# Attention scores on reversed query rows: the relative bias moves from TensorE to VectorE, two kinds of transfer move to GpSimd's queue, and every weight split is done in halves

## What is computed

```python
xn = _rmsnorm(h, norm_mix_g)
p_rw, q, c_kv, iq, ik, iw, gates = _split(xn @ w_in, IN_SPLITS)
# RWKV branch: each token's projection is mixed with that of the token before it
prev = jnp.pad(p, ((0, 0), (1, 0), (0, 0)))[:, :T]
z = p + (prev - p) * shift_mix
# attention branch, for each block of 128 queries
score = einsum('bqhs,bqh->bqs', relu(einsum('bqhd,bsd->bqhs', qi, ik)), wi)
score = where(allowed, score, -inf)            # chunks of 64 tokens
top_s, idx = lax.top_k(score, 64)
logits = einsum('bqhr,bqkr->bqhk', ql, c_sel) * SA_SCALE
logits = logits + rel_bias[_rel_bucket(idx - tq)]
pr = softmax(where(valid, logits, -inf))
o = (pr @ c_sel) @ w_uv                        # 16 heads of width 64
g_a, g_b = split(sigmoid(gates))               # stored for a later stage
```

## Time and profile before

| what | value |
|---|---|
| median of three runs | 4171.05 us |
| the profiled execution's own time | 4167.72 us |
| its span, first to last instruction | 4165.9 us |
| TensorE matmuls busy | 3637.2 us (87%) |
| VectorE busy | 2181.1 us (52%) |
| ScalarE busy | 1689.0 us (41%) |
| GpSimd busy | 301.2 us (7%) |
| mean granted TensorE clock | 0.923 of full speed |

### The profile page before, as it was taken

How to read it: one execution, slowest core, us unless ns; L and a number is a source line. 1 busy time by engine, 2 the same in 40 slices (tenths; PEclk the granted TensorE clock), 3 DMA queues, 4 the chain that set the end, 5 groups by cost and what they waited for, 6 DMA issues and landing times. The chain is left out here.

```text
span 4165.9 us, 50794 instructions
## 1 busy us (share of the span) xinstructions
PE 3637.2 (87%) x20602; PEld 3105.0 (75%) x20602; DVE 2181.1 (52%) x2490; ACT 1689.0 (41%) x2027; POOL 301.2 (7%) x115
## 2 busy tenths in 40 slices
PE   7877893444588999999999999999799999798999
PEld 6655772334476799998888999888588887686777
DVE  4533434544455367685554435555567875345444
ACT  4332331111233334674444444444455543233663
POOL 0000000000000178100000000000012220000000
PEclk9988995666699999999999999999899999899999
DMA  5333561010244445555555556555343434254434
GB/s 195 138 113 130 188 213 34 9 30 10 89 155 175 162 152 184 176 176 187 208 191 190 203 192 258 198 199 191 137 174 136 139 130 155 97 188 154 151 139 154
DMA packets 112890, 635.26 MB, mean 152 GB/s; under 512 B 21575, under 2 KB 28133, under 8 KB 40655
## 3 DMA queue, kind: packets, MB, share of 16 engines
q1 hardware_dynamic: 107760, 622.12, 42.3%
q10 hardware_dynamic: 4287, 8.71, 0.5%
q0 software_dynamic: 672, 2.11, 0.2%
HBM read 609.50 MB, written 19.96 MB: 151 GB/s over the span
## 5 line engine op out<-in xcount | busy, mean ns | idle before, releaser
L218 DVE TENSOR_TENSOR lo_w<-ring,hi_w 128x2048 fp32r<-128x2048 f32 x500 | 1144.2, 2294 | 1177.3 <-ACT hi_w L213 1173.0
L213 ACT CAST hi_w<-ring 128x2048 fp32r<-128x2048 f32 x540 | 1028.3, 1910 | 1085.1 <-DMA ring<-in_wstream 1018.7
L1505 PE MATMUL PS<-hi_x,hi_w 128*128 128x256 f32 x2048 | 578.1, 282 | 2.5 <-ACTq L1619 2.1
L1505 PE MATMUL PS<-hi_x,lo_w 128*128 128x256 f32 x2048 | 580.0, 283 | 0.0
L1505 PE MATMUL PS<-lo_x,hi_w 128*128 128x256 f32 x2048 | 572.3, 279 | 0.0
L1531 PE MATMUL PS<-hi_w,lo_g 128*128 128x512 f32 x1024 | 405.5, 396 | 0.0
L1531 PE MATMUL PS<-hi_w,hi_g 128*128 128x512 f32 x1024 | 401.5, 392 | 0.9 <-issue 0.9
L1531 PE MATMUL PS<-lo_w,hi_g 128*128 128x512 f32 x1024 | 399.4, 390 | 0.0
L1505 PEld LDWEIGHTS PS<-hi_x,hi_w 128*128 128x128 f32 x2048 | 389.0, 190 | 3.0 <-issue 2.9
L1505 PEld LDWEIGHTS PS<-lo_x,hi_w 128*128 128x128 f32 x2048 | 385.9, 188 | 0.0
L1505 PEld LDWEIGHTS PS<-hi_x,lo_w 128*128 128x128 f32 x2048 | 385.9, 188 | 0.0
(11 more groups left out here) (491 smaller groups left out, 5515.9 us busy)
## 6 DMA issues: line engine op xcount, KB each, us to landing
ring<-in_wstream SPq DMA_DIRECT2D x540, 1024.0 KB, 4.8
other_G<-staged SPq DMA_DIRECT2D x32, 256.0 KB, 6.0
hot<-other_G SPq DMA_DIRECT2D x8, 1024.0 KB, 6.9
x<-in_x SPq DMA_DIRECT2D x2, 2048.0 KB, 12.7
gates_dram<-gst ACTq DMA_DIRECT2D x8, 512.0 KB, 6.1
gsb<-gates_dram SPq DMA_DIRECT2D x1, 4096.0 KB, 13.2
x_dram<-x SPq DMA_DIRECT2D x2, 2048.0 KB, 11.3
x<-x_dram SPq DMA_DIRECT2D x2, 2048.0 KB, 9.1
```

The costliest lines, as they stand in the source:

```text
L213: a.copy(hi_w[s][:], ring[s][:]).then_inc(S(f"hi{s}"), 1)
L218: v.tensor_tensor(lo_w[s][:], ring[s][:], hi_w[s][:].bitcast(F32), ALU.subtract).then_inc(S(f"lo{s}"), 1)
L1505: m = nc.tensor.matmul(PS[:, s, 0:T], wa[s][:, k * P:(k + 1) * P], xa[:, k, :], start=(k == 0 and p == 0), stop=(k == KC - 1 and p == 2))
```

## The change

Six edits, in words:

1. The query rows stay reversed through the whole attention. The query, index-query and output turns, transposes against `ident` before, become matmuls against `anti`; the index weights are reversed by one small matmul (`iwr`), and the constant `limit` is written in reversed order. The bias tile then has the same row order as the scores. `qk` issues two matmuls in place of four and no longer waits for the bias; `maxima` waits for it and adds it, then adds the penalty in a second instruction.
2. The two shift transfers of m = 4 to 10 go from ScalarE's queue to GpSimd's.
3. The eight gate stores go from ScalarE's queue to GpSimd's.
4. `split_hi` and `split_lo` work in two halves of 1024 columns in all 540 units; VectorE or GpSimd starts on the first half when ScalarE has cast it. TensorE waits for both as before.
5. `PAIR` starts one iteration later (15 for 14) and ends one later (32 for 31); the output turns of each tile follow one iteration later (26 and 35).
6. In iteration 12 the second `relus` stands behind the `hi` split of unit 15 in place of ahead of it.

```diff
+    HALF = UNIT // 2
     def split_hi(a, g, s):
         a.wait_ge(S(f"landed{s}"), g * 16 + 16)
-        a.copy(hi_w[s][:], ring[s][:]).then_inc(S(f"hi{s}"), 1)
+        a.copy(hi_w[s][:, 0:HALF], ring[s][:, 0:HALF]).then_inc(S(f"hi{s}"), 1)
+        a.copy(hi_w[s][:, HALF:UNIT], ring[s][:, HALF:UNIT]).then_inc(S(f"hi{s}"), 1)
     def split_lo(v, g, s):
-        v.wait_ge(S(f"hi{s}"), g + 1)
-        v.tensor_tensor(lo_w[s][:], ring[s][:], hi_w[s][:].bitcast(F32), ALU.subtract).then_inc(S(f"lo{s}"), 1)
+        v.wait_ge(S(f"hi{s}"), g * 2 + 1)
+        v.tensor_tensor(lo_w[s][:, 0:HALF], ring[s][:, 0:HALF], hi_w[s][:, 0:HALF].bitcast(F32), ALU.subtract)
+        v.wait_ge(S(f"hi{s}"), g * 2 + 2)
+        v.tensor_tensor(lo_w[s][:, HALF:UNIT], ring[s][:, HALF:UNIT], hi_w[s][:, HALF:UNIT].bitcast(F32), ALU.subtract)\
+            .then_inc(S(f"lo{s}"), 1)
...
-    PAIR = {14: 0, 15: 1, 16: 2, 18: 3, 19: 4, 20: 5, 21: 6, 22: 7, 23: 8, 24: 9, 26: 10, 27: 11, 28: 12, 29: 13, 30: 14, 31: 15}
+    PAIR = {15: 0, 16: 1, **{16 + p: p for p in range(2, 10)}, **{17 + p: p for p in range(10, 16)}}
...
                 if p >= 4:
-                    sp.wait_ge(S("qk"), p - 3)
+                    sp.wait_ge(S("qk_read"), p - 3)
...
-                        m = nc.tensor.transpose(PS[:, b, k * P:(k + 1) * P], qr[:, i, tt, k * P:(k + 1) * P], ident[:])
+                        m = nc.tensor.matmul(PS[:, b, k * P:(k + 1) * P], qr[:, i, tt, k * P:(k + 1) * P], anti[:], start=True, stop=True)
...
             def qk(p):
-                t.wait_ge(S(f"bias_in{p % 4}"), 16 * (p // 4) + 16)
                 for e in range(2):
                     r = slice(64 * e, 64 * e + 64)
-                    nc.tensor.matmul(PS[:, 3 + e, 0:w], anti[:], bias[:, p % 4, e, 0:w], start=True, stop=False)
-                    m = nc.tensor.matmul(PS[:, 3 + e, 0:w], qT[r, j, tt * P:(tt + 1) * P], kT[r, j, 0:w], start=False, stop=True)
+                    m = nc.tensor.matmul(PS[:, 3 + e, 0:w], qT[r, j, tt * P:(tt + 1) * P], kT[r, j, 0:w], start=True, stop=True)
...
-            def shifted(m, src):
-                a.dma_start(prev[1:P, s, :, 0:n], src[0:P - 1, :, 0:n]).then_inc(S(f"prev{s}"), 16)
-                a.dma_start(prev[0:1, s, 1, 0:n], src[P - 1:P, 0, 0:n]).then_inc(S(f"prev{s}"), 16)
...
         @block.gpsimd
         def _(g):
             g.wait_ge(S("vv_sb"), 2)
             for m in range(4, 11):
+                n = WIDTH.get(m, 512)
+                s, src = m % 2, zs if m == 4 else part_of(m - 5)
                 if m >= 6:
                     g.wait_ge(S("mixed"), m - 5)
-                g.memset(prev[0:1, m % 2, 0, :], 0.0).then_inc(S("prev_zero"), 1)
+                g.memset(prev[0:1, s, 0, :], 0.0).then_inc(S("prev_zero"), 1)
+                g.wait_ge(S("rkv_in"), m - 3)
+                g.dma_start(prev[1:P, s, :, 0:n], src[0:P - 1, :, 0:n]).then_inc(S(f"prev_in{s}"), 16)
+                g.dma_start(prev[0:1, s, 1, 0:n], src[P - 1:P, 0, 0:n]).then_inc(S(f"prev_in{s}"), 16)
+            for c in range(8):
+                g.wait_ge(S("gate_sb"), c + 1)
+                g.dma_start(gates[:, :, c * 512:(c + 1) * 512].rearrange("t p f -> p t f"), gst[:, c % 2])\
+                    .then_inc(S(f"gate_out{c % 2}"), 16)
...
             def maxima(p):
                 v.wait_ge(S("qk"), p + 1)
-                v.tensor_tensor(prob[:, :, 0:w], PS[:, 3:5, 0:w], pen[:, tt, 0:w].unsqueeze(1).broadcast_to((P, 2, w)), ALU.add)
+                v.wait_ge(S(f"bias_in{p % 4}"), 16 * (p // 4) + 16)
+                v.tensor_tensor(prob[:, :, 0:w], PS[:, 3:5, 0:w], bias[:, p % 4, :, 0:w], ALU.add)
                 v.drain().then_inc(S("qk_read"), 1)
+                v.tensor_tensor(prob[:, :, 0:w], prob[:, :, 0:w], pen[:, tt, 0:w].unsqueeze(1).broadcast_to((P, 2, w)), ALU.add)
+                v.drain()
                 v.tensor_reduce(dst_[:, 0, :], prob[:, :, 0:w], X, ALU.max)
```

More of the change, by code:

```diff
@@ L132, in recycle @@
     def recycle():
-        kept = ("landed", "hi", "lo", "norm_", "unit_used", "psum_free", "turn_hi", "turned", "x_back", "mix_in", "prev_in")
+        kept = ("landed", "hi", "lo", "norm_", "unit_used", "psum_free", "turn_hi", "turned", "x_back", "prev_in", "gate_out")
         old = [n for n in sems if not n.startswith(kept)]
@@ L433, in build @@
     iw = sb("iw", (P, NT, 8))
+    iwr = sb("iwr", (P, NT, 8))
     prev = over("prev", (P, 2, NT, 512), F32, bump[0])
@@ L522, in turn_c @@
                         nc.tensor.transpose(PS[:, 3, (2 * tt + k) * P:(2 * tt + k + 1) * P], cn[:, tt, k * P:(k + 1) * P], ident[:])
-                    m = nc.tensor.transpose(PS[:, 4, tt * P:(tt + 1) * P], ik2[:, tt, :], ident[:])
-                m.then_inc(S("c_ps"), 1)
+                    nc.tensor.transpose(PS[:, 4, tt * P:(tt + 1) * P], ik2[:, tt, :], ident[:])
+                t.wait_ge(S("dsa_in"), 80)
+                nc.tensor.matmul(PS[:, 4, T:T + 16], anti[:], iw[:].rearrange("p t h -> p (t h)"), start=True, stop=True)\
+                    .then_inc(S("c_ps"), 1)
             def keys(i):
@@ L553, in turn_iq @@
                     for k in range(4):
-                        m = nc.tensor.transpose(PS[:, 3 + tt, k * P:(k + 1) * P], iqr[:, tt, k * P:(k + 1) * P], ident[:])
+                        m = nc.tensor.matmul(PS[:, 3 + tt, k * P:(k + 1) * P], iqr[:, tt, k * P:(k + 1) * P], anti[:], start=True, stop=True)
                 m.then_inc(S("iq_ps"), 1)
@@ L590, in qk @@
                     t.wait_ge(S("q_T"), 1)
-                if j == 3 and tt == 0:
+                if j == 4 and tt == 0:
                     t.wait_ge(S("q_T"), 2)
@@ L631, in turn_o @@
                 for k in range(8):
-                    m = nc.tensor.transpose(PS[:, 3 + k // 4, (k % 4) * P:(k % 4 + 1) * P], oo[:, k * P:(k + 1) * P], ident[:])
+                    m = nc.tensor.matmul(PS[:, 3 + k // 4, (k % 4) * P:(k % 4 + 1) * P], oo[:, k * P:(k + 1) * P], anti[:], start=True, stop=True)
                 m.then_inc(S("o_ps"), 1)
@@ L655, in _ @@
                     turn_q((u - 13) // 4)
-                if u in (25, 34):
-                    turn_o((u - 25) // 9)
+                if u in (26, 35):
+                    turn_o((u - 26) // 9)
                 if u in PAIR:
@@ L759, in _ @@
                     elif m <= 10:
-                        src = zs if m == 4 else part_of(m - 5)
-                        arrive(m, src, "rkv_in")
-                        shifted(m, src)
+                        arrive(m, zs if m == 4 else part_of(m - 5), "rkv_in")
                     else:
@@ L769, in _ @@
                     a.copy(ikT[:], PS[:, 4, 0:T])
+                    a.copy(iwr[:].rearrange("p t h -> p (t h)"), PS[:, 4, T:T + 16])
                     a.drain().then_inc(S("c_T"), 1)
@@ L785, in _ @@
                     a.drain().then_inc(S("iq_T"), 1)
-                if u in (11, 12):
-                    relus(u - 11)
+                if u == 11:
+                    relus(0)
                 if u in (13, 17):
@@ L795, in _ @@
                     turned_p(PAIR[u - 1])
-                if u in (24, 33):
-                    out_o((u - 24) // 9)
                 if u in (25, 34):
-                    turned_o((u - 25) // 9)
+                    out_o((u - 25) // 9)
+                if u in (26, 35):
+                    turned_o((u - 26) // 9)
                 if u + 3 < WU:
                     hi(u + 3)
+                if u == 12:
+                    relus(1)
                 if u in PAIR:
@@ L842, in scores @@
                 v.wait_ge(S("idx_relu"), tt + 1)
-                v.tensor_scalar(score[:, 0:w], relu[:, 0, 0:w], iw[:, tt, 0:1], None, ALU.mult)
+                v.wait_ge(S("c_T"), 1)
+                v.tensor_scalar(score[:, 0:w], relu[:, 0, 0:w], iwr[:, tt, 0:1], None, ALU.mult)
                 for h in range(1, 8):
                     v.drain()
-                    v.scalar_tensor_tensor(out=score[:, 0:w], in0=relu[:, h, 0:w], scalar=iw[:, tt, h:h + 1],
+                    v.scalar_tensor_tensor(out=score[:, 0:w], in0=relu[:, h, 0:w], scalar=iwr[:, tt, h:h + 1],
                                            in1=score[:, 0:w], op0=ALU.mult, op1=ALU.add)
```

16 lines of the change are left out of this document (4 added, 12 removed).

## The result

The changed kernel takes **4061.1 us** (median of four runs, 4055.4 to 4063.9) against 4169.5 for the kernel before in the same set (4163.7 to 4178.8): a ratio of 0.9736, interval 0.9715 to 0.9757, or 108 us less. Forecast were 4080 and a range from 4064 to 4118.

What follows compares the result with a forecast made beforehand. TensorE was taken to idle behind slow 127-row shift transfers on ScalarE's queue, at a lowered clock; 15 - 9 + 64 + 18 + 4 - 1 = 91 us gained from 4167.7 gives 4076.7, with the median 4080; range 4064 to 4118.

Steps and rivals of the forecast that it cites:

- Waits: TensorE's waits in the changed stage: 76.4 us go except about 12 at the front, so 64 gained.
- GpSimd's rows are the only ones of its queue: Shift transfers on GpSimd: reason for taking a 7 us landing from its 256 KB rows (3.4 to 7.3).
- Clock: TensorE's half-clock time after five stalls that go: 18 us gained, between 12 and 24.
- Bias products: Attention pairs on TensorE: 64 bias records go, 20.6 us busy; 15 us gained, between 10 and 20.
- Reversing products: Five groups of eight transposes become float32 products: 40 x 0.22 = 9 us lost, up to 14 at half clock.
- Halves: Splits in halves: first chain shortens 0.8 us at five stage starts, 4 gained; the rest lies beside TensorE's work.
- cover of 0.6 us: VectorE's longer attention pair: a unit and the pair before cover it by 0.6 us, so costed at nothing.
- The sign against the forecast: Later stages: forecast falls if groups, L1505 above all, begin to wait for a split; no size given.
- Stores and the end: Gate stores moved to GpSimd: ScalarE's saving hidden, the last ends the block; 1 us lost, between -1 and 3.
- one engine still: Rival, chance 0.06: GpSimd's 127-row shifts still use one DMA engine, landing about 28 us; 87 of 91 lost, 4166 us.
- One engine, and slower: Rival, chance 0.04: GpSimd's shifts on one engine land at about 40 us; 123 lost against 91, 4203 us.
- The pair's chain: Rival, chance 0.13: VectorE's add and halves take 2 us more, 1.4 show at some thirteen pairs, 18 in all; 4098 us.

Runs made afterwards that it cites:

- m = 4 sent by tile: Changed kernel with the m = 4 shift from GpSimd as two transfers of 127 x 288, one for each token tile: 4052.4 us, ratio 0.9699.
- the shifts alone: Kernel before with only the two shift transfers of each RWKV part issued by GpSimd: 4082.5 us, ratio 0.9797.
- edit 1: Kernel before with shifts on GpSimd, plus reversed rows and the bias on VectorE, old `PAIR` and whole splits: 4075.8 us, ratio 0.9769.
- whole splits: Every split whole again: in the changed kernel 4072.8 us (0.9768); in the changed kernel with shifts on ScalarE as 112 and 15 rows 4067.1 (0.9745).
- m = 5 in columns: Changed kernel with the m = 5 shift from GpSimd in two transfers of 256 columns each: 4079.1 us, ratio 0.9764.

## Why the prediction was right, and where it was wrong

- **Waits**: forecast 64 gained, measured 59. The landing of 7 us was right (5.6, and no VectorE wait from m = 5 on). The step that failed is "GpSimd's rows are the only ones of its queue", read as if one landing held for all seven shifts: m = 4 has another form. It cost 3 us at 174 us, where VectorE's operation was held, and 1.6 at 199; with m = 4 sent by tile the waits are 12.7, and the forecast had 12.
- **Clock**: forecast 18, measured 21 (the shifts alone), inside 12 to 24.
- **Bias products**: forecast 15, between 10 and 20. This is the step that failed most. I counted the records that go, 20.6 us busy, less their overlap, and not what they kept apart: each stood between the two heads' products, which now run together. With the reversing products measured at 4.6, the 16.6 us of edit 1 make the bias term 21.
- **Reversing products**: forecast 9, measured 4.6. A group of eight takes 1.71 us from its first start to the next instruction's where eight transposes took 0.79, so 0.92 for each of five groups. I took 0.34 for a product from the earlier trace rows; here it is 0.21. The row had been read over a fall of the clock. Two stretches of it (columns as in the earlier trace rows; ten records, then some twenty, two to a product):

```profile
1460.45:1461.67 1.22, 1.22 (x10) 1.22 (x11) 1.07 (x7) 0.00 (x0) 0.00 (x0) 1.00 0.00 0
1461.99:1465.90 3.91, 3.91 (x21) 3.74 (x20) 3.46 (x20) 0.00 (x0) 0.00 (x0) 0.59 0.00 0
```

  At the full clock a product of the same row takes 2 x 0.12 us, and 40 x (0.24 - 0.12) is 4.8, what was measured.
- **Halves**: forecast 4, measured 10 to 13. The step was "beside TensorE's work": some 5 us come through VectorE's queue in this stage, and some 6 in the later stages by a path that stays open. Without the halves the cover of 0.6 us does not hold everywhere (the 2.57 and 1.37 above); in the changed kernel no later pair waits, as forecast. The sign against the forecast that it names for the later stages, L1505 waiting for a split, did show, but small: that group waits 2.9 us for GpSimd's splits where it waited 0.4.
- **Stores and the end**: 1 was to be lost; the wait at the end of the stage is 7.7 us where it was 7.8, so nothing was.
- **Rivals**: "one engine still" fell for six shifts and held for the seventh. "One engine, and slower" fell. The pair's chain did not show in the changed kernel. It shows a little elsewhere: 3 us at the front with the old places of the pairs, and 5 at three later pairs with whole splits.

Added up from the traces: 59 of waits, 19.5 of clock (10.9 in the units, 8.6 between them), 16.6 of edit 1, 2.2 more in the products between the units and 6.3 outside the stage are the 104 that the spans differ by, where the forecast had 91. Bias and reversing together were 6 in the sum and are 16.6 in the runs: 10.6 of the 12.8 that the forecast lacks. They take 4080 to 4069, and all terms take it to 4067, inside the range. The last 6 us are the spread between runs: I had added 3.3 for the median before, and the profiled execution after stands 2.8 above its median. So that the time fell below the low end, and not just above it, is partly chance; that the bias term was sized too small is not.

The range allowed some 14 us either way for all terms together. Three missed to the same side: the bias just beyond its 20, the reversing products and the halves with no bound stated on that side.

## What to carry to other kernels

Look at the number of rows of a slow transfer before moving it to another queue: cut off the rows that spoil divisibility by 16, and, from GpSimd, keep each row one piece. When a product of full height goes from between two of half height, count the overlap that the two gain, not only the product's own time. Before taking a duration from a row of a trace, look at the granted clock inside that row, not only at its edges. Work of a second engine that is cut in halves can pay through the order of that engine's queue, even where the bottleneck did not wait for that work itself.

## What the runs showed of the hardware that was not expected

- A GpSimd transfer of 127 rows in two pieces each that lie apart in the target: 3.6 to 3.8 us to issue (0.53 to 0.86 for the others), in the changed kernel 945 packets of 16 B, and the data over one engine at 22 GB/s (0.18 MB in 8 us). The slow issue was seen with pieces of 512, 576, 1024 and 1152 B.
- During such an issue a VectorE operation with one tensor in (`tensor_scalar`, 128x256) took 3.25 to 3.40 us in place of 0.30, in the six kernels in which it began 0.49 or 0.50 us behind the start of the issue, and ended 0.09 behind its end. In the three in which it began 0.42 us behind (shifts alone, reversed rows on top of them, whole splits) it took 0.29 to 0.30. With m = 5 in columns a `tensor_scalar` of 128x2 that began 1.20 us behind the first issue took 2.42 in place of 0.17, and the split behind it 2.35 in place of 1.22. The 128x256 `tensor_tensor` that began 1.03 us behind took 0.42 to 0.43, its usual time. So the hold is seen to begin with one kind of operation, and what brings it on was not tried.
- Float32 products of 64 rows on the two halves of the array overlap wholly: 0.70 us for both heads as for one.
